# Second batch of state-space table products issued in the norm after the first FFN instead of in that FFN's last chunk

## The chip, the cores and the metric

The kernel runs on one core of a Trainium2 chip. The metric is the device time of one execution in microseconds; lower is better. Within 0.2% (2.4 us of 1207.69) counts as no change.

## The reference, cut to what matters

A decoder of four layers works on 256 positions of 1024 channels in float32. Each layer is a mixer and a norm, then an FFN and a norm. The mixers are attention, a state-space layer (S5), pooling, attention. The change touches the end of layer 0 (its FFN and the norm behind it) and the start of layer 1 (S5).

```
for i in range(DEPTH):
    m = mixer_i(h)                       # i = 1: s5_mixer
    h = layer_norm(DN_ALPHA * h + m, ln_g[i, 0], ln_b[i, 0])
    h = layer_norm(DN_ALPHA * h + swiglu(h, w1[i], w3[i], w2[i]), ln_g[i, 1], ln_b[i, 1])

# s5_mixer: u = x @ w_in, 64 groups of 16 channels, 64 complex states per group
#   h_t = lam * h_(t-1) + B u_t ;  y_t = Re(C h_t) + D u_t ;  gelu ; GLU with w_glu
```

## The kernel before

Each float32 matmul against weights is done as three products of reduced-precision halves. A weight tile of 128x1024 (512 KB) comes by DMA into one of four `raw` buffers, ScalarE (ACT) rounds it to its high half (`hi`), VectorE (DVE) subtracts to get the low half (`lo`), and TensorE (PE) uses both. The tiles are numbered in the order of use. SyncE (SP) issues their loads in this order in one program: the load of tile c waits until the low half of tile c-4 is made (`w_lo`). All engines run fixed programs, written by hand and synchronised by semaphores; nothing is scheduled at run time.

S5 works on blocks of eight positions. What happens inside a block is one 128x128 matrix (a Toeplitz block) per group, and these 64 matrices are computed by the kernel from the S5 parameters while the FFN of layer 0 runs. The last step of that is `m_half(h)`, for h = 0 and 1: 64 pairs of small products on PE make the first block rows of 32 groups in two PSUM banks; ACT copies both to `Msb[h]` (h = 0 in `slot3`, h = 1 in `lam`); `s5_diagonal` on DVE adds the D term and raises `m_d`. Then each of the eight block rows is stored to DRAM (`toep`) from Msb, 4 x 2 DMAs for each row: GpSimd (POOL) issues 40 of them (rows 0 to 4), SP issues 24 (rows 5 to 7). SP does this inside its sequence of tile loads: after the load of the tile S0+5 it waits for `m_d`, issues its 24 stores, and only then the loads of tiles S0+6 and S0+7 (S0 is the first of S5's eight `w_in` tiles) and then the moves of u described below. Much later the blocks are loaded back as `toepA` and `BT`.

The norm behind the FFN (n = 1, function `ln`) handles the 256 positions as two halves m = 0 and 1 of 128. DVE adds the residual from the accumulator banks (banks 0 and 1 for m = 0, banks 2 and 3 for m = 1), takes statistics and writes `x_tm`; PE transposes it (`turn_x`) into banks 4 to 7; ACT and DVE make the high and low halves `xboth`. S5 begins inside the norm: PE multiplies tiles S0 and S0+1 with m = 0, has then to wait for the second half's `x_tm`, and goes on with `turn_x(n, 1, (0, 1))`. The remaining tiles S0+2 to S0+7 follow (`u_tile(i)`, tile S0+i; i from 4 on writes banks 2 and 3). The result u is regrouped by four DMAs for each half h (two from ACT, two from SP, called `u_moves`), then `u_turned` goes on with it.

In the trace the lines are: L1783 and L1784 the products of `m_half` on PE, L696 its copies on ACT, L1366, L1370, L1372 `s5_diagonal` on DVE, L569 and L440 the stores on POOL and SP, L431 the loads of the `w_in` tiles on SP, L595 and L974 the high and low halves of a tile, L1571 `turn_x`, L1936, L1937, L1942 the products of `u_tile`, L389 `u_moves`, L795 and L1386 the copies behind them, L1955 `u_turned`, L1967 the next batch of 64 products.

Of the kernel before, what the change touches and what calls it, by code (L numbers as in the profile page):

```python
# [23 lines left out]
ALU = mybir.AluOpType  # L24
# [3 lines left out]
P = 128  # L28
# [7 lines left out]
FCH = D_FF // P  # L36
# [61 lines left out]
def build(nc, t, layers=DEPTH, last_ffn=True):  # L98
# [38 lines left out]
    with ExitStack() as ctx:  # L137
# [3 lines left out]
        def sem(name):  # L141
            return ctx.enter_context(nc.semaphore(name))
# [122 lines left out]
        def up_half(n, m):  # L265

            return bank[4 + m] if after_fox(n) else bank[m]

        def nth(n, m, b):

            return 8 * (n + 1) + 4 * m + b + 1
# [9 lines left out]
        later_landed, x_landed, bglu_landed = sem("later_landed"), [sem("x0_landed"), sem("x1_landed")], sem("bglu_landed")  # L281
        ones_set, bhi_sb, blo_sb = sem("ones_set"), sem("bhi_sb"), sem("blo_sb")
        up1_lo, up3_lo, up1_sum = sem("up1_lo"), sem("up3_lo"), sem("up1_sum")
        sub_done, zeros_set = sem("sub_done"), sem("zeros_set")
        var_ready, std_ready = sem("var_ready"), sem("std_ready")
        xn_ready = [sem("xn0_ready"), sem("xn1_ready")]
# [82 lines left out]
        def _(sp):  # L369
# [54 lines left out]
            for c in range(RAW, n_tiles):  # L424
                sp.wait_ge(w_lo, c - RAW + 1)
                for dst, src in LATER.get(c - KC - RAW, []):
                    sp.dma_start(dst, src).then_inc(later_landed, 16)
                if T1 <= c < T1 + KC:

                    h, k = (c - T1) // 4, T1 + 2 * ((c - T1) % 4)  # L430
                    sp.dma_start(raw[:, c % RAW, :].rearrange("p (k d) -> p k d", k=2),  # L431
                                 t["w"][k:k + 2, :, h * HALF:(h + 1) * HALF].rearrange("k p d -> p k d")).then_inc(raw_landed[c % RAW], 16)
                else:
                    sp.dma_start(raw[:, c % RAW, :], t["w"][tile_at(c)]).then_inc(raw_landed[c % RAW], 16)
                if c == T1 + RAW + 1:
                    sp.wait_ge(m_d, 1)
                    for s in range(5, STEP):
                        for j in range(4):
                            for h in range(2):
                                sp.dma_start(*toep_block(s, j, h)).then_inc(m_st_sp, 16)  # L440
                if c == T1 + 4 + RAW:
                    u_moves(0)
                if c == T1 + KC + RAW - 1:
                    u_moves(1)
                    toep_moves(T1)
# [5 lines left out]
        def _(pool):  # L451
# [87 lines left out]
            for l in range(layers):  # L539
                kind = MIXERS[l]  # L540
                if kind == "fox":


                    if l > 0:
                        pool.wait_ge(xn_ready[1], 2 * 2 * l)
                        nc.gpsimd.tensor_copy(
                            qa_of(1)[HD:KQ, :, :], cst[HD:KQ, C_HOT:C_HOT + HEADS].unsqueeze(2).to_broadcast([HEADS, HEADS, SEQ])
                        ).then_inc(qa_rows, 1)
                    if l == 0 and layers > 1:
                        s5_parameters()  # L550
                        step(nc.gpsimd.memset(slot[2][:, 0:D], 0.0))
                        for k in range(8):
                            pool.dma_start(t["toep"][:, k * D:(k + 1) * D], slot[2][:, 0:D]).then_inc(zero_st, 16)
                        pool.wait_ge(zero_st, 16 * 8)
                for k in range(2):

                    if kind == "s5" and k == 0:
                        pool.wait_ge(y_ps, 4)
                    if n > 0:
                        pool.wait_ge(xn_ready[1], 2 * n)  # L560
                    for q in range(2):
                        pool.dma_start(gb[:, q, :], t["ln_row"][q, n].partition_broadcast(P)).then_inc(gb_landed, 16)  # L562
                    if n == 1 and layers > 1:
                        s5_turns()
                        pool.wait_ge(m_d, 1)
                        for s in range(5):
                            for j in range(4):
                                for h in range(2):
                                    pool.dma_start(*toep_block(s, j, h)).then_inc(m_st, 16)  # L569
                    n += 1  # L570

# [2 lines left out]
        def _(act):  # L574
# [38 lines left out]
            def opening():  # L613

                for b in range(4):
                    for m in range(TM):
                        high(-1, m, b)
                    hi_to(min(b, 2))

            def ln(n, ahead, table, last_gate=None):  # L620

                nc.scalar.preload_act_table(ACT.Sqrt)
# [13 lines left out]
                    nc.scalar.preload_act_table(table)  # L636
                for b in range(4):
                    high(n, 1, b)

            def ffn(l, n):  # L640
                T0 = starts[l] + MIX_TILES[MIXERS[l]]
# [47 lines left out]
                        act.wait_ge(wb_ps, 2 * b + i + 1)  # L689
                        nc.scalar.copy(BT[:, 8 * b + 4 * i:8 * b + 4 * i + 4, :], bank[6 + i][:, :].rearrange("p (g n) -> p g n", g=4)).then_inc(bt_sb, 1)  # L690

                def m_half(h):

                    for i in range(2):
                        act.wait_ge(m_ps, 2 * h + i + 1)
                        nc.scalar.copy(Msb[h][:, 4 * i:4 * i + 4, :], bank[6 + i][:, :].rearrange("p (g n) -> p g n", g=4)).then_inc(m_sb, 1)  # L696

                s5_here = l == 0 and layers > 1
                act.wait_ge(up_ps, l + 1)
                silu_half(0)  # L700
# [10 lines left out]
                for c in range(2, FCH):  # L711
                    chunk(c)
                    if s5_here and 5 <= c < 13:
                        bt_block(c - 5)
                    if s5_here and c >= FCH - 2:
                        m_half(c - FCH + 2)
                split_to(top)

            def fox(l, f):
# [231 lines left out]
        def _(dve):  # L951
# [29 lines left out]
            def residual(n, m, j, src):  # L981

                if n > 0:
                    dve.wait_ge(xn_ready[m], 2 * n)
                cols = slice(j * HALF, (j + 1) * HALF)
                step(V.scalar_tensor_tensor(x_tm[:, m, cols], x_tm[:, m, cols], ALPHA, src, ALU.mult, ALU.add))

            def measure(m, j):
# [19 lines left out]
            def ln(n, last_tile, ahead, glu=None):  # L1008
# [68 lines left out]
                if between:  # L1077
                    for b in range(4):
                        low(n, 1, b)
                    lo_to(ahead)  # L1080

            def ffn(l, n):
# [73 lines left out]
                for c in range(2, FCH):  # L1156
                    chunk(c)
                if tables_here:
                    s5_diagonal()
                split_to(top)  # L1160

            def fox(l, f):
# [195 lines left out]
                        else:  # L1358
                            mark(ins)

            def s5_diagonal():

                tD = slot[0][:, 0:SEQ].rearrange("p (g c) -> p g c", g=16)
                dve.wait_ge(tables, 1)
                dve.wait_ge(turns, 1)
                mark(V.tensor_tensor(tD, dcol[:, :].unsqueeze(2).to_broadcast([P, 16, GC]),  # L1366
                                     cst[:, C_ID16:C_ID16 + GC].unsqueeze(1).to_broadcast([P, 16, GC]), ALU.mult))
                dve.wait_ge(m_sb, 4)
                marked()
                mark(V.tensor_tensor(Msb[0][:, :, 0:GC], Msb[0][:, :, 0:GC], tD[:, 0:8, :], ALU.add))  # L1370
                marked()
                V.tensor_tensor(Msb[1][:, :, 0:GC], Msb[1][:, :, 0:GC], tD[:, 8:16, :], ALU.add).then_inc(m_d, 1)  # L1372

            def s5(l, n):
                T0 = starts[l]
# [180 lines left out]
        def _(pe):  # L1556
# [132 lines left out]
            def zero_products(b, times):  # L1689

                for _ in range(times):
                    mm(bank[b][:, 0:SEQ], turn_sb[:, 0, 0:P], turn_sb[:, 0, 0:SEQ], start=True, stop=True)

            def ffn(l, n):
                T0 = starts[l] + MIX_TILES[MIXERS[l]]
                E0 = FCH * l
# [71 lines left out]
                            ins = nc.tensor.transpose(bank[6 + i][:, g * P:(g + 1) * P], BT[:, 8 * b + 4 * i + g, :], ident)  # L1768
                        ins.then_inc(wb_ps, 1)

                def m_half(h):

                    pe.wait_ge(tables, 1)
                    pe.wait_ge(bt_sb, 16)
                    if h == 1:
                        pe.wait_ge(m_sb, 2)
                    for i in range(2):
                        b = 2 * h + i
                        for q in range(4):
                            for j in range(4):  # L1780
                                g = 16 * j + 4 * b + q
                                lhs = slot[1][:, g * GC:g * GC + 32]
                                mm(bank[6 + i][32 * j:32 * j + 32, q * P:q * P + GC], lhs, CA[:, g, :], start=True, stop=True)  # L1783
                                ins = mm(bank[6 + i][32 * j:32 * j + 32, q * P + GC:(q + 1) * P], lhs,  # L1784
                                         CT[:, g, 0:STEP - 1, :].rearrange("p d c -> p (d c)"), start=True, stop=True)
                        ins.then_inc(m_ps, 1)

                s5_here = l == 0 and layers > 1
                pe.wait_ge(w_lo, T0 + 4)
                up_both(0).then_inc(up_ps, 1)  # L1790
# [7 lines left out]
                for c in range(3, FCH):  # L1798
                    up1(c)
                    up3(c)  # L1800
                    if c < FCH - 3:
                        down(c - 1)
                    if s5_here and 5 <= c < 13:
                        bt_block(c - 5)
                    if s5_here and c >= FCH - 2:
                        m_half(c - FCH + 2)
                down(FCH - 4)
                t, h = T0 + T_FFN - 3, FCH - 3

# [114 lines left out]
            def s5(l, n):  # L1924
# [115 lines left out]
                for m in range(TM):  # L2040
                    for i in range(2):
# [4 lines left out]
                        if i == 0:  # L2046
                            turn_x(n, m, (2, 3))
                    if m == 0:
                        turn_x(n, 1, (0, 1))
                for i in range(2, KC):  # L2050
                    u_tile(i)
                pe.wait_ge(ug0_sb, 1)
                pe.wait_ge(ug1_sb, 1)
# [220 lines left out]
```

## Time and profile before

| | us |
|---|---|
| median of 3 runs | 1207.69 (1207.59 to 1207.75) |
| the profiled execution | 1208.1 |
| its span, first to last instruction | 1206.3 |
| PE busy | 1172.1 (97% of the span) |
| DVE busy | 881.8 (73%) |
| ACT busy | 635.0 (53%) |
| POOL busy | 145.3 (12%) |

The profiled execution lies 0.4 us above the median, and 1.8 us of it lie outside the span. The profile lists instructions with start and duration on each engine, and for an engine that sat idle, what released it. Times in the rows are us from the start of the span. PE's matmuls overlap, so the distance between the starts of two of them is what one costs.

### The profile page before, as it was taken

Reading aid. Unit: us, or ns where it says so; the run is one execution under the profiler, and the core shown is the slowest. Engines: PE = TensorE matmul, PEld = TensorE weight load, DVE = VectorE, ACT = ScalarE, POOL = GpSimd, SP = SyncE. Lnnn points to the kernel's source line nnn. Section 1 sums busy time; section 2 is a strip of 40 time slices with the busy share of each in tenths; the row PEclk is TensorE's granted clock in tenths of the full one; section 3 lists DMA queues with packets and bytes.
Section 4 is the critical chain, followed back from the end, with each engine's and each line's share of the span. In section 5 each row is a group of like instructions: output and inputs, shape, how many; then the busy total and the mean of one; then the engine's idle time right before and its main releaser. Section 6 shows DMA issues by size and latency. Waiting matters only on the chain.

```text
span 1206.3 us, 18971 instructions
## 1 busy us (share of the span) xinstructions
PE 1172.1 (97%) x7386; PEld 1004.9 (83%) x7386; DVE 881.8 (73%) x1412; ACT 635.0 (53%) x1069; POOL 145.3 (12%) x187
## 2 busy tenths in 40 slices
PE   9999999999988999999998999999999999999996
PEld 7887899999967778888887888888878977888885
DVE  6779889889776677665668887666686767766655
ACT  5766445454435366555554556554538654654552
POOL 0640079101650000000000000000010000000000
PEclk9999999999999999999999999999999999999998
DMA  6684465655588556756654647666636433866550
GB/s 232 209 294 158 155 194 158 192 164 186 182 173 235 190 174 205 231 183 189 196 185 142 207 138 246 193 189 193 189 126 205 128 106 122 261 193 192 182 168 35
DMA packets 66513, 220.17 MB, mean 183 GB/s; under 512 B 11124, under 2 KB 12660, under 8 KB 65912
## 3 DMA queue, kind: packets, MB, share of 16 engines
q1 hardware_dynamic: 60536, 202.47, 53.1%
q0 software_dynamic: 4736, 14.55, 4.1%
q10 hardware_dynamic: 1152, 1.93, 0.7%
q8 instruction: 59, 0.97, 0.3%
q14 instruction: 30, 0.25, 0.1%
HBM read 210.28 MB, written 7.60 MB: 181 GB/s over the span
## 4 chain that ended last, share of the span: by engine, by line
PE 85%; DVE 9%; ACT 3%; DMA 2%; issue 1%; SPq 0%; ACTq 0%; DVEq 0%
PE bank L1599 18%; PE bank L1602 9%; PE bank L1614 9%; PE bank L1616 9%; PE bank L1620 9%; PE bank L1591 5%; PE bank L1593 5%; PE bank L1592 5%; PE bank L1651 4%; PE bank L1706 4%; DVE wlo L974 1%; PE bank L1571 1%; DVE ext L974 1%; DMA slot<-slot 1%; DVE x_tm L1032 1%
## 5 line engine op out<-in xcount | busy, mean ns | idle before, releaser
L974 DVE TENSOR_TENSOR wlo<-raw,whi 128x1024 fp32r<-128x1024 f32 x227 | 285.1, 1263 | 51.2 <-ACT whi L595 48.8
L595 ACT ACTIVATE whi<-raw 128x1024 fp32r<-128x1024 f32 x227 | 239.1, 1058 | 46.9 <-DMA raw<-in_w 26.8
L974 DVE TENSOR_TENSOR ext<-raw,ext 128x1024 fp32r<-128x1024 f32 x142 | 173.7, 1230 | 36.4 <-ACT ext L595 33.8
L1599 PE MATMUL bank<-xboth,whi 128*128 128x512 f32 x480 | 170.0, 397 | 0.0
L1599 PE MATMUL bank<-xboth,ext 128*128 128x512 f32 x480 | 168.7, 394 | 0.0
L595 ACT ACTIVATE ext<-raw 128x1024 fp32r<-128x1024 f32 x142 | 149.1, 1058 | 22.9 <-DMA raw<-in_w 16.2
L1591 PE MATMUL bank<-xboth,whi 128*128 128x256 f32 x496 | 142.1, 286 | 0.0
L1592 PE MATMUL bank<-xboth,whi 128*128 128x256 f32 x496 | 140.3, 283 | 0.0
L1593 PE MATMUL bank<-xboth,wlo 128*128 128x256 f32 x496 | 140.3, 283 | 0.0
L1602 PE MATMUL bank<-xboth,ext 128*128 128x256 f32 x480 | 124.6, 280 | 0.0
L1602 PE MATMUL bank<-xboth,wlo 128*128 128x256 f32 x480 | 124.2, 279 | 0.0
L1599 PEld LDWEIGHTS bank<-xboth,whi 128*128 128x128 f32 x480 | 88.4, 188 | 17.6 <-issue 0.3
L1599 PEld LDWEIGHTS bank<-xboth,ext 128*128 128x128 f32 x480 | 88.4, 188 | 16.4
L1591 PEld LDWEIGHTS bank<-xboth,whi 128*128 128x128 f32 x496 | 94.9, 191 | 1.7 <-issue 1.2
L1592 PEld LDWEIGHTS bank<-xboth,whi 128*128 128x128 f32 x496 | 95.0, 191 | 0.5
L1593 PEld LDWEIGHTS bank<-xboth,wlo 128*128 128x128 f32 x496 | 94.9, 191 | 0.0
L1602 PEld LDWEIGHTS bank<-xboth,wlo 128*128 128x128 f32 x480 | 90.5, 189 | 5.0
L1602 PEld LDWEIGHTS bank<-xboth,ext 128*128 128x128 f32 x480 | 90.4, 188 | 5.0
L663 ACT COPY cosT<-bank 128x256 f32<-128x256 f32 x60 | 22.3, 372 | 131.0 <-PE bank L1599 130.6
L1117 DVE TENSOR_TENSOR silu<-bank,cosT 128x256 f32<-128x256 f32 x60 | 25.4, 423 | 89.4 <-ACT cosT L663 89.2
L562 POOL DMA_DIRECT2D slot<-in_ln_row x16 | 8.6, 543 | 542.4 <-DVE x_tm L1044 472.4
L1614 PE MATMUL bank<-whi,hhi 128*128 128x512 f32 x196 | 61.0, 392 | 0.0
(396 smaller groups left out, 2329.7 us busy)
## 6 DMA issues: line engine op xcount, KB each, us to landing
raw<-in_w SPq DMA_DIRECT2D x370, 512.0 KB, 4.3
slot<-in_ln_row POOLq DMA_DIRECT2D x16, 512.0 KB, 5.0
toep<-slot POOLq DMA_DIRECT2D x8, 512.0 KB, 9.2
toepA<-toep SPq DMA_DIRECT2D x2, 1024.0 KB, 10.0
BT<-toep SPq DMA_DIRECT2D x2, 1024.0 KB, 7.3
slot<-in_s_B SPq DMA_DIRECT2D x2, 512.0 KB, 5.4
slot<-in_s_C SPq DMA_DIRECT2D x2, 512.0 KB, 4.6
x_tm<-in_x SPq DMA_DIRECT2D x1, 512.0 KB, 5.1
```

The lines of the kernel that those rows point to most:

```text
L595: nc.scalar.activation(hi_of(c), raw[:, c % RAW, :], ACT.Copy).then_inc(w_hi, 1)
L974: V.tensor_tensor(lo_of(c), raw[:, c % RAW, :], hi_of(c).bitcast(F32), ALU.subtract).then_inc(w_lo, 1)
L1591: mm(dst, wh, bhi[:, kc, :], start=(i == 0), stop=False)
L1592: mm(dst, wh, blo[:, kc, :], start=False, stop=False)
L1593: ins = mm(dst, wl, bhi[:, kc, :], start=False, stop=(i == len(chunks) - 1))
L1599: return mm(dst[:, :], hi_of(c)[:, kc * P:(kc + 1) * P], xboth[:, kc, :, :].rearrange("p a t -> p (a t)"), start=kc == 0, stop=kc == KC - 1)
L1602: return mm(dst[:, 0:SEQ], lo_of(c)[:, kc * P:(kc + 1) * P], xhi[:, kc, :], start=False, stop=False)
L1614: mm(banks[2 * m + j][:, :], a_hi[:, cols], hi_of(c)[:, j * HALF:(j + 1) * HALF], start=first, stop=False)
L1616: mm(banks[2 * m + j][:, :], a_hi[:, cols], lo_of(c)[:, j * HALF:(j + 1) * HALF], start=False, stop=False)
L1620: ins = mm(banks[2 * m + j][:, :], a_lo[:, cols], hi_of(c)[:, j * HALF:(j + 1) * HALF], start=False, stop=last)
L1651: return mm(banks[b][:, :], (a_lo if lo_act else a_hi)[:, cols], (lo_of if lo_w else hi_of)(c)[:, half], start=False, stop=stop)
L1706: return mm(out, x[:, kc, m * P:(m + 1) * P], w[:, 0:4, kc * P:(kc + 1) * P], start=start, stop=stop)
```

## The change

`m_half(1)` and all that hangs on it move. On PE its 64 pairs of products leave the last chunk of the FFN and stand between the last product of tile S0+1 with m = 0 and the transposes of the second half. They write banks 2 and 3 instead of 6 and 7, and wait for a new semaphore, `acc_read`, which DVE raises when it has read the second half's sums out of these banks. On ACT the two copies move behind the second of the four copies of `xboth` of the second half. On DVE the addition of the D term for h = 1 moves to the end of the norm. POOL's 40 stores are ordered by h, the first 20 behind `m_d` 1 and the other 20 behind `m_d` 2. SP's 24 stores wait for `m_d` 2, which is now raised by the moved addition; before, `m_d` 1 was raised when both halves were done. `u_tile(4)` also waits for the copies on ACT (`m_sb` 4).

```diff
+        def m_bank(h, i):
+
+            return bank[6 + i] if h == 0 else bank[2 + i]
...
                 if c == T1 + RAW + 1:
-                    sp.wait_ge(m_d, 1)
+                    sp.wait_ge(m_d, 2)
                     for s in range(5, STEP):
                         for j in range(4):
                             for h in range(2):
...
                         s5_turns()
-                        pool.wait_ge(m_d, 1)
-                        for s in range(5):
-                            for j in range(4):
-                                for h in range(2):
+                        for h in range(2):
+                            pool.wait_ge(m_d, h + 1)
+                            for s in range(5):
+                                for j in range(4):
                                     pool.dma_start(*toep_block(s, j, h)).then_inc(m_st, 16)
...
                 for b in range(4):
                     high(n, 1, b)
+                    if n == 1 and layers > 1 and b == 1:
+                        m_half(1)
...
-                    if s5_here and c >= FCH - 2:
-                        m_half(c - FCH + 2)
+                    if s5_here and c == FCH - 2:
+                        m_half(0)
...
+                if n == 1 and m == 1 and layers > 1:
+                    V.scalar_tensor_tensor(x_tm[:, m, cols], x_tm[:, m, cols], ALPHA, src, ALU.mult, ALU.add).then_inc(acc_read, 1)
+                    dve.wait_ge(acc_read, j + 1)
+                    return
...
                     for b in range(4):
                         low(n, 1, b)
+                    if n == 1 and layers > 1:
+                        s5_diagonal(1)
                     lo_to(ahead)
...
+            def m_half(h):
+
+                pe.wait_ge(tables, 1)
+                pe.wait_ge(bt_sb, 16)
+                for i in range(2):
+                    if h == 1:
+                        pe.wait_ge(acc_read, i + 1)
...
                     if m == 0:
+                        m_half(1)
                         turn_x(n, 1, (0, 1))
                 for i in range(2, KC):
+                    if i == 4:
+                        pe.wait_ge(m_sb, 4)
                     u_tile(i)
```

On PE, between tile S0+1 (its halves are in `far_hi` and `far_lo`) and the transposes of the second half, the order before is:

```order
L1942 MATMUL bank0<-far_hi,xboth 128x512 [waits xT_ready]
L1942 MATMUL bank0<-far_hi,xboth 128x512
L1571 MATMUL bank4<-cst,x_tm 128x128 [waits xT_ready,xn1_ready]
L1571 MATMUL bank4<-cst,x_tm 128x128
L1571 MATMUL bank5<-cst,x_tm 128x128 [waits xT_ready]
```

And with the change (the lines are twelve further on in its file here):

```order
L1954 MATMUL bank0<-far_hi,xboth 128x512 [waits xT_ready]
L1954 MATMUL bank0<-far_hi,xboth 128x512
L1718 MATMUL bank2<-slot3,slot1 32x16 [waits acc_read,bt_sb,tables]
L1719 MATMUL bank2<-CT,slot1 32x112
...
L1718 MATMUL bank3<-slot3,slot1 32x16
L1719 MATMUL bank3<-CT,slot1 32x112
L1583 MATMUL bank4<-cst,x_tm 128x128 [waits xT_ready,xn1_ready]
L1583 MATMUL bank4<-cst,x_tm 128x128
```

The 128 small products, 64 pairs, now stand between the two, in banks 2 and 3.

On DVE, the additions before stand together ahead of the norm, and the end of the norm (the low halves of `xboth`, then those of tiles S0+2 to S0+5) has none:

```order
L1366 TENSOR_TENSOR slot0<-dcol,cst 128x256 [waits turns,tables,hlo_ready]
L1370 TENSOR_TENSOR slot3<-slot3,slot0 128x8x16 [waits dve_own,m_sb]
L1372 TENSOR_TENSOR lam<-lam,slot0 128x8x16 [waits dve_own]
L974 TENSOR_TENSOR wlo<-raw,whi 128x1024 [waits w_hi]
...
L996 TENSOR_TENSOR xboth<-bank7,xboth 128x2x128 [waits xhi_ready]
L974 TENSOR_TENSOR wlo<-raw,whi 128x1024 [waits w_hi] x4
L1380 COPY slot0<-bank1 128x512 [waits w_used]
```

With the change:

```order
L1380 TENSOR_TENSOR slot0<-dcol,cst 128x256 [waits turns,tables,hlo_ready]
L1384 TENSOR_TENSOR slot3<-slot3,slot0 128x8x16 [waits dve_own,m_sb]
L981 TENSOR_TENSOR wlo<-raw,whi 128x1024 [waits w_hi]
...
L1007 TENSOR_TENSOR xboth<-bank7,xboth 128x2x128 [waits xhi_ready]
L1384 TENSOR_TENSOR lam<-lam,slot0 128x8x16 [waits dve_own,m_sb]
L981 TENSOR_TENSOR wlo<-raw,whi 128x1024 [waits w_hi] x4
L1392 COPY slot0<-bank1 128x512 [waits w_used]
```

The addition for h = 1, into `lam`, is now behind the last low half of `xboth` and ahead of tile S0+2's low half.

On SP nothing changes places; with the change its rows from the six loads S0 to S0+5 to the first moves of u are (the first and the last of the 24 stores shown):

```order
L436 DMA raw<-in_w 128x2x512 [waits w_lo] x6
L445 DMA toep<-slot3 16x8x48 [waits m_d]
L445 DMA toep<-lam 16x8x48
...
L445 DMA toep<-lam 16x8x16
L436 DMA raw<-in_w 128x2x512 [waits w_lo] x2
L439 DMA raw<-in_w 128x1024 [waits w_lo]
L394 DMA slot4<-slot0 16x8x256 [waits u1_sb]
L394 DMA slot4<-slot0 16x8x256
```

What moved is the point of the program at which its `m_d` wait is met: it is now released by the addition into `lam` at its new place.

## Rows read from the trace of the kernel before

**Rows 1.** Page, part 4: shares of the chain that ended last.

```profile
PE 85%; DVE 9%; ACT 3%; DMA 2%; issue 1%; SPq 0%; ACTq 0%; DVEq 0%
```

**Rows 2.** Timeline of PE (start us, us, engine, line, operation), the batch h = 1 and what follows.

```profile
323.81 0.26 PE L1783 MATMUL bank<-slot 128*32 128x16 f32 x7
...
326.07 0.73 PE L1614 MATMUL bank<-whi,hhi 128*128 128x512 f32 x2
...
330.31 0.39 PE L1651 MATMUL bank<-whi,h4hi 128*128 128x512 f32 x1
```

**Rows 3.** Timelines of DVE and ACT, end of the FFN to start of the norm.

```profile
325.88 1.23 DVE L974 TENSOR_TENSOR wlo<-raw,whi 128x1024 fp32r<-128x1024 f32 x1
...
327.88 0.29 DVE L1372 TENSOR_TENSOR lam<-lam,slot 128x128 f32<-128x128 f32 x1
...
332.55 0.68 DVE L986 SCALAR_TENSOR_TENSOR x_tm<-x_tm,bank 128x512 f32<-128x512 f32 x1
...
325.76 1.05 ACT L696 COPY lam<-bank 128x512 f32<-128x512 f32 x2
329.18 1.06 ACT L595 ACTIVATE whi<-raw 128x1024 fp32r<-128x1024 f32 x1 [2.37 <-PE bank L1620]
```

**Rows 4.** Timelines of PE and ACT in the norm and in the tiles behind it.

```profile
341.19 0.63 PE L1942 MATMUL bank<-far_hi,xboth 128*128 128x512 f32 x2
344.03 0.66 PE L1571 MATMUL bank<-cst,x_tm 128*128 128x128 f32 x4 [2.21 <-DVE x_tm L1044]
...
349.49 0.50 PE L1936 MATMUL bank<-whi,xboth 128*128 128x512 f32 x1 [0.77 <-DVE wlo L974]
...
360.54 0.39 PE L1936 MATMUL bank<-whi,xboth 128*128 128x512 f32 x1
...
365.53 0.61 PE L1942 MATMUL bank<-whi,xboth 128*128 128x512 f32 x2
...
347.13 0.66 ACT L605 ACTIVATE xboth<-bank 128x256 fp32r<-128x256 f32 x2 [1.96 <-PE bank L1571]
```

**Rows 5.** Timeline of SP's queue (start, time to issue, transfer).

```profile
333.07 0.74 SPq L440 DMA_DIRECT2D toep<-slot  x1
...
342.49 0.43 SPq L440 DMA_DIRECT2D toep<-lam  x1
...
352.07 0.94 SPq L431 DMA_DIRECT2D raw<-in_w  x2
...
356.02 1.34 SPq L389 DMA_DIRECT2D slot<-slot  x2
```

**Rows 6.** Timelines of DVE and ACT: halves of tiles S0+2 to S0+6.

```profile
348.22 4.62 DVE L974 TENSOR_TENSOR wlo<-raw,whi 128x1024 fp32r<-128x1024 f32 x4
...
357.41 1.23 DVE L974 TENSOR_TENSOR wlo<-raw,whi 128x1024 fp32r<-128x1024 f32 x1 [1.42 <-ACT whi L595]
...
356.31 1.06 ACT L595 ACTIVATE whi<-raw 128x1024 fp32r<-128x1024 f32 x1 [1.79 <-DMA raw<-in_w]
```

**Rows 7.** The chain that ended last, in order of time, 356 to 384 us.

```profile
356.73 9.71 DMA slot<-slot
...
367.57 1.95 PE bank L1955 x32
...
370.15 3.11 PE bank L1967 x64
...
382.82 1.89 PE bank L1967 x64
```

**Rows 8.** Windows (us, then busy time of PE, PEld, DVE, ACT, POOL, PE's granted clock, DMA share, GB/s).

```profile
342.00:344.00 2.00, 0.00 (x0) 0.00 (x0) 1.96 (x6) 0.29 (x1) 2.00 (x5) 1.00 0.69 131
...
370.00:372.00 2.00, 2.00 (x49) 1.92 (x52) 0.40 (x1) 0.79 (x2) 0.00 (x0) 0.66 1.22 138
372.00:374.00 2.00, 2.00 (x28) 1.61 (x21) 0.94 (x2) 1.26 (x3) 0.00 (x0) 0.50 1.06 201
...
1200.00:1202.00 2.00, 0.00 (x0) 0.00 (x0) 1.90 (x5) 0.29 (x1) 0.00 (x0) 0.52 0.23 94
```

More of the change, by code:

```diff
@@ L283, in build @@
         up1_lo, up3_lo, up1_sum = sem("up1_lo"), sem("up3_lo"), sem("up1_sum")
+        acc_read = sem("acc_read")
         sub_done, zeros_set = sem("sub_done"), sem("zeros_set")
@@ L618, in opening @@
                     hi_to(min(b, 2))
+            def m_half(h):
+                for i in range(2):
+                    act.wait_ge(m_ps, 2 * h + i + 1)
+                    nc.scalar.copy(Msb[h][:, 4 * i:4 * i + 4, :], m_bank(h, i)[:, :].rearrange("p (g n) -> p g n", g=4)).then_inc(m_sb, 1)
             def ln(n, ahead, table, last_gate=None):
@@ L690, in bt_block @@
                         nc.scalar.copy(BT[:, 8 * b + 4 * i:8 * b + 4 * i + 4, :], bank[6 + i][:, :].rearrange("p (g n) -> p g n", g=4)).then_inc(bt_sb, 1)
[L692 to L696, printed above, removed]
                 s5_here = l == 0 and layers > 1
@@ L1158, in ffn @@
                 if tables_here:
-                    s5_diagonal()
+                    s5_diagonal(0)
                 split_to(top)
@@ L1359, in s5_tables, with s5_diagonal @@
                             mark(ins)
-            def s5_diagonal():
+            def s5_diagonal(h):
                 tD = slot[0][:, 0:SEQ].rearrange("p (g c) -> p g c", g=16)
[L1364 to L1368, printed above, removed]
+                if h == 0:
+                    dve.wait_ge(tables, 1)
+                    dve.wait_ge(turns, 1)
+                    mark(V.tensor_tensor(tD, dcol[:, :].unsqueeze(2).to_broadcast([P, 16, GC]),
+                                         cst[:, C_ID16:C_ID16 + GC].unsqueeze(1).to_broadcast([P, 16, GC]), ALU.mult))
+                dve.wait_ge(m_sb, 2 * h + 2)
                 marked()
-                mark(V.tensor_tensor(Msb[0][:, :, 0:GC], Msb[0][:, :, 0:GC], tD[:, 0:8, :], ALU.add))
-                marked()
-                V.tensor_tensor(Msb[1][:, :, 0:GC], Msb[1][:, :, 0:GC], tD[:, 8:16, :], ALU.add).then_inc(m_d, 1)
+                V.tensor_tensor(Msb[h][:, :, 0:GC], Msb[h][:, :, 0:GC], tD[:, 8 * h:8 * h + 8, :], ALU.add).then_inc(m_d, 1)
             def s5(l, n):
@@ L1692, in zero_products, with m_half @@
                     mm(bank[b][:, 0:SEQ], turn_sb[:, 0, 0:P], turn_sb[:, 0, 0:SEQ], start=True, stop=True)
+            def m_half(h):
+                pe.wait_ge(tables, 1)
+                pe.wait_ge(bt_sb, 16)
+                for i in range(2):
+                    if h == 1:
+                        pe.wait_ge(acc_read, i + 1)
+                    b = 2 * h + i
+                    for q in range(4):
+                        for j in range(4):
+                            g = 16 * j + 4 * b + q
+                            lhs = slot[1][:, g * GC:g * GC + 32]
+                            mm(m_bank(h, i)[32 * j:32 * j + 32, q * P:q * P + GC], lhs, CA[:, g, :], start=True, stop=True)
+                            ins = mm(m_bank(h, i)[32 * j:32 * j + 32, q * P + GC:(q + 1) * P], lhs,
+                                     CT[:, g, 0:STEP - 1, :].rearrange("p d c -> p (d c)"), start=True, stop=True)
+                    ins.then_inc(m_ps, 1)
             def ffn(l, n):
@@ L1769, in bt_block @@
                         ins.then_inc(wb_ps, 1)
[L1771 to L1786, printed above, removed]
                 s5_here = l == 0 and layers > 1
@@ L1804, in ffn @@
                         bt_block(c - 5)
-                    if s5_here and c >= FCH - 2:
-                        m_half(c - FCH + 2)
+                    if s5_here and c == FCH - 2:
+                        m_half(0)
                 down(FCH - 4)
```

## The prediction

> **What bounds the kernel now.** I first read the page's chain that ended last: PE holds most of it [rows 1]. So an instruction taken from a place where PE is busy is worth its time, as long as what follows is ready earlier too, and a wait added on PE costs its full length. The change touches only the stretch from 323 to about 373 us, so I next read the timelines of that stretch engine by engine, and last its chain. Three things are to be seen. At 323.81 us the batch h = 1 runs with PE busy before and after it [rows 2]. In the norm PE stands still for 2.21 us before the transposes of the second half, since it needs DVE's x_tm [rows 4]. And SP, between its loads of tiles S0+5 and S0+6, is occupied with its 24 stores from 333.07 to 352.07 us [rows 5].
>
> **The batch leaves the FFN.** From its first product to the next matmul it takes 326.07 - 323.81 = 2.26 us [rows 2]. Is what follows ready that much earlier? The last tile of the FFN is wanted at 330.31, then 328.05; its low half ends at 325.88 + 1.23 = 327.11 and doesn't depend on the batch [rows 2, 3]. 0.94 us are left. The norm's first step on DVE, at 332.55, follows on the halves of S0 and S0+1, and the first of these was released by a PE product at 329.18 [rows 3], so it comes 2.26 us earlier too. **-2.26 us**, for everything up to the transposes.
>
> **The batch enters the norm.** The last two products of S0+1 with m = 0 run from 341.19 to 341.82; such a product is 0.39 long, so they start about 0.23 apart and make room at 341.65; the transposes start at 344.03 [rows 2, 4]. That is 2.38 us for 2.26 us of work. The sums of the second half have been read by then, because what PE waits for at 344.03 lies several DVE steps behind them. So **0** on PE. If the cover were gone it would cost 2.26 us, and the bounds here are 0 and about +0.2 (start of a small product after a large one).
>
> **ACT's copies.** They take 1.05 us [rows 3] and stand ahead of the xboth copy of 347.13, before which ACT idled 1.96 us [rows 4]. **0.** Without this cover 1.05 would be paid.
>
> **DVE's addition.** 0.29 us [rows 3]. Before, it lay in an idle of DVE ahead of the norm. Now it stands right ahead of the low halves from 348.22, of which the first releases PE at 349.49 after a wait [rows 4, 6]. **+0.29 us.** Tile S0+2 then starts at 349.49 - 2.26 + 0.29 = 347.52, and I call -1.97 us the gain so far.
>
> **SP's wait.** This is the term that decides. m_d 2 is raised at the end of the norm: 348.22 - 2.26 + 0.29 = 346.25, against a wait that was met without delay at 333.07 before [rows 5, 6]. Queued behind it on SP are the 24 stores, the loads of tiles S0+6, S0+7 and the next one, and u_moves. The 24 issues took 19.0 us before: the first 7 took 9.42 us, to 342.49, and the other 17 took 9.58 us, 0.564 each, to 352.07 [rows 5]. The first seven stood right behind the loads of S0+4 and S0+5, which will be over by 346 us. POOL's issues go on beside SP's in both. I take the second rate: 24 x 0.564 = 13.5 us. The bounds are the bare 0.43 and a gap of 0.05 (11.5 us) and the whole 19.0 us.
> The load of S0+6 is then issued at 346.25 + 13.5 = 359.8. Before, from its issue at 352.07 to the end of its low half at 357.41 + 1.23 = 358.64 it took 6.57 us [rows 5, 6]. So the tile is ready at 366.4. PE wants it at 360.54 - 1.97 = 358.6 [rows 4]. **PE waits 7.8 us** where before the tile had 1.9 us to spare. Tiles S0+6 and S0+7 take 5.45 us, from 360.54 to 366.0 (the last two start at 365.53, 0.23 apart) [rows 4], so PE is through at 371.8, and u_turned starts at about 372.0. Before it started at 367.57, because it waited for the moves of u [rows 7]. **+4.4 us** at this point. From there S5 is one chain, and nothing in it is set by a clock of its own; SP's second u_moves, the loads of toepA and POOL's stores all stand within the same shift.
>
> **TensorE's clock.** After 2.2 us without a matmul the granted clock stayed at 1.00 (2.4 GHz) [rows 8]. After PE's last matmul, with nothing for several us, it fell to half (1.2 GHz) by 1200 to 1202 us [rows 8]. And before the S5 chain it fell for some 3.4 us between 370 and 374 us, behind a short idle and small transposes [rows 8]; there 64 products took 3.11 us against 1.89 us later [rows 7]. A wait of 7.8 us should let it fall. For up to 3.4 us PE then works at half speed and loses up to 1.7 us. On the other side the idle ahead of u_turned is gone, and I assume that the fall at 370 us goes with it, -1.2 us (3.11 - 1.89). **+0.5 us** net; the bounds are -1.2 and +1.7.
> The Trainium skill, page "TensorE: Matmul & The Clock Gate", section "HAM oscillation — how this bites in real kernels", says that a wait for a DMA between two groups of matmuls can bring the clock down to half, so that the next group starts slow. By that rule the tiles behind the wait are slow and the sum ends at +4.9 or above; without it, at +3.2 to +4.4. The trace agrees as far as its idle at the very end shows the fall, but no wait for a tile of this length stands in it.
>
> **Sum.** -2.26 and +0.29 are inside the +4.4 already: 4.4 + 0.5 = +4.9 us. On the span that is 1206.3 + 4.9 = 1211.2, with 1.8 us outside it 1213.0 for the profiled execution, and since that one lay 0.4 above the median, 1207.69 + 4.9 = **1212.6 us**.
>
> **The rivals.**
> 1. *The stores issue faster and the clock is kind.* At 0.48 us each the tile is 2.0 us less late, +2.4 us at u_turned; if also no slow stretch follows, or the old one vanishes without a new one, +1.2. That is 1208.9 to 1210.1, and mostly within 0.2%. For it: seventeen issues included only one long one. Against it: POOL will be storing its largest blocks just then. 0.14.
> 2. *The tile is not late, and the change gains.* Then PE keeps -1.97 us: 1205.7 us. It decides at the point where SP gets through its 24 stores by 358.6 - 6.57 = 352.0, in 5.7 us or 0.24 us each. The fastest row is 0.43 [rows 5]. It would take a route of the tile that is far shorter than 6.57 us, or a u_turned that is released so much sooner that it pays. Nothing in the profile speaks for it beyond my own reading of the order. 0.08.
> 3. *The moves of u end last.* u_moves is issued behind three tile loads, at about 361.3, and if it takes its 9.71 us again [rows 7] and the copy behind it 1.1, u_turned starts at 372.1 to 373, +4.6 to +5.5, and with slow products more; some 1213 us. For it: the row of 9.71 us is on the chain now. Against it: in it the moves from ACT and more tile loads ran at the same time, and these will be apart. 0.13.
> 4. *SP's issues are as slow as before, 19.0 us:* +5.5 on top, 1218.1 us. For it: the first seven. Against it: no tile load runs beside them. 0.05.
> The forecast, SP held at a middling rate, has 0.60.
>
> **How the numbers follow.** Cases 3, 4 and the forecast are slower by more than 0.2% (73 + 5 = 0.78), case 1 is mostly no change (0.14), case 2 is faster (0.08). The range runs from the middle of case 1, 1209.3, to near case 4, 1217.0; that leaves out case 2, half of 1 and most of 4.
>
> **What would show it.** The batch L1783/L1784 (under new line numbers) in the idle before the transposes, and these at 341.8 us: right on the first two steps. The addition at 346 us, SP's first store directly behind it and the load of S0+6 near 360 us: right on SP. PE idle before the first product of u_tile(6), some 8 us, released by DVE's low half, and a granted clock of half in the window behind it. u_turned near 372 to 374 us. I would be wrong if the load of S0+6 is issued before 353 us, or if the 24 issues take a third of the time that I give them.

## The result and the profile after

The changed kernel takes 1216.26 us (median of 6 runs, 1215.5 to 1218.74), the kernel before 1207.64 us (6 runs, 1203.97 to 1207.97): ratio 1.0077, 95% interval 1.0060 to 1.0093. It is slower by 8.6 us. Forecast were 1212.6 us and a range of 1209.3 to 1217.0. The profiled execution took 1216.19 us with a span of 1214.4, 8.1 above that of before.

The page's chain that ended last (answers to [rows 1]); SP's queue has come into it:

```profile
PE 84%; DVE 9%; ACT 3%; issue 1%; SPq 1%; DMA 1%; DVEq 0%; ACTq 0%
```

The timeline of PE (answers to [rows 2, 4]):

```profile
338.66 0.63 PE L1954 MATMUL bank<-far_hi,xboth 128*128 128x512 f32 x2
339.22 0.26 PE L1718 MATMUL bank<-slot 128*32 128x16 f32 x7
...
341.50 0.66 PE L1583 MATMUL bank<-cst,x_tm 128*128 128x128 f32 x4
...
347.16 0.50 PE L1948 MATMUL bank<-whi,xboth 128*128 128x512 f32 x1 [0.97 <-DVE wlo L981]
...
368.62 0.79 PE L1948 MATMUL bank<-whi,xboth 128*128 128x512 f32 x1 [10.30 <-DVE wlo L981]
...
376.18 1.95 PE L1967 MATMUL bank<-cst,slot 32*128 32x32 f32 x32
```

The batch fills the idle of the norm, and the transposes behind it start 2.53 us earlier than before with no wait. Tile S0+2 starts 2.33 us earlier. Then PE stands still for 10.30 us ahead of S0+6, and u_turned, the last row, starts 8.61 us later than in [rows 7].

DVE, ACT and POOL (answers to [rows 3, 6]):

```profile
330.04 0.68 DVE L997 SCALAR_TENSOR_TENSOR x_tm<-x_tm,bank 128x512 f32<-128x512 f32 x1
...
345.69 0.28 DVE L1384 TENSOR_TENSOR lam<-lam,slot 128x128 f32<-128x128 f32 x1
346.26 10.32 POOL L574 DMA_DIRECT2D toep<-lam  x20 [7.80 <-DVE lam L1384]
...
366.25 1.06 ACT L600 ACTIVATE whi<-raw 128x1024 fp32r<-128x1024 f32 x1 [14.10 <-DMA raw<-in_w]
367.34 1.23 DVE L981 TENSOR_TENSOR wlo<-raw,whi 128x1024 fp32r<-128x1024 f32 x1 [13.73 <-ACT whi L600]
```

SP's queue (answers to [rows 5]), the 24 stores L445 and the load of S0+6, L436:

```profile
346.00 0.35 SPq L445 DMA_DIRECT2D toep<-slot  x1
...
352.96 1.09 SPq L445 DMA_DIRECT2D toep<-lam  x1
354.10 1.66 SPq L445 DMA_DIRECT2D toep<-slot  x1
...
361.82 0.43 SPq L445 DMA_DIRECT2D toep<-lam  x1
362.29 0.94 SPq L436 DMA_DIRECT2D raw<-in_w  x2
```

The first store follows at once on the addition of 345.69. While POOL issues its second twenty, from 346.26 to 356.58, SP's issues take up to 1.66 us; from 357.56 on they take 0.43. The 24 together take 362.29 - 346.00 = 16.3 us.

The chain that ended last shows the same stretch as one path, and what comes at its end (answers to [rows 7]):

```profile
362.29 3.94 DMA raw<-in_w
366.25 1.06 ACT whi L600
367.34 1.24 DVE wlo L981
368.62 0.79 PE bank L1948
...
389.82 3.53 PE bank L1979 x64
```

The windows (columns as in [rows 8]):

```profile
350.00:352.00 2.00, 2.00 (x10) 1.68 (x9) 0.51 (x1) 0.44 (x1) 2.00 (x5) 1.00 0.91 139
...
362.00:364.00 2.00, 0.00 (x0) 0.00 (x0) 0.00 (x0) 0.00 (x0) 0.00 (x0) 0.61 0.31 39
...
370.00:372.00 2.00, 2.00 (x6) 1.54 (x5) 0.58 (x1) 0.90 (x1) 0.00 (x0) 0.50 1.13 124
372.00:374.00 2.00, 2.00 (x8) 1.59 (x8) 1.81 (x2) 0.75 (x2) 0.00 (x0) 0.83 0.94 317
...
390.00:392.00 2.00, 2.00 (x44) 1.85 (x40) 1.87 (x5) 0.27 (x2) 0.00 (x0) 0.50 0.00 0
```

The granted clock is still 1.00 (2.4 GHz) in the first windows of the wait, falls to half (1.2 GHz) from 362 us on, and is back between 372 and 374 us: S0+6 and S0+7 take from 368.62 to 376.1, 7.5 us against 5.45 before. It falls once more at 390 us.

### The profile page after: what moved, and what is told of

Its sections match the earlier page's. It is cut to its first block, busy times and chain, and to the rows that moved or that the text cites. A ratio compares the mean times of both kernels' runs of the same rounds, so it can differ in the third digit from the quotient of the medians.

```text
span 1214.4 us, 18973 instructions
## 1 busy us (share of the span) xinstructions
PE 1173.3 (97%) x7386; PEld 1005.6 (83%) x7386; DVE 881.6 (73%) x1412; ACT 635.2 (52%) x1069; POOL 145.4 (12%) x187
## 4 chain that ended last, share of the span: by engine, by line
PE 84%; DVE 9%; ACT 3%; issue 1%; SPq 1%; DMA 1%; DVEq 0%; ACTq 0%
PE bank L1611 18%; PE bank L1614 9%; PE bank L1626 9%; PE bank L1628 9%; PE bank L1632 9%; PE bank L1603 5%; PE bank L1605 5%; PE bank L1604 5%; PE bank L1663 4%; PE bank L1735 4%; DVE wlo L981 2%; SPq L445 1%; PE bank L1583 1%; DVE ext L981 1%; DMA raw<-in_w 1%
```

## The experiments

The theory: all of the loss comes from SP's `m_d` wait at the end of the norm, which holds the load of S0+6 behind 24 issues; the place of the batch on PE is a gain. Rivals: the batch in the norm costs something itself; the wait for the tile is harmless and the clock behind it is the cost; the moves of u end last.

The table has each kernel's median, and from its profiled execution the start of tile S0+2, PE's idle ahead of S0+6, the start of u_turned, and as a last mark the start of the late batch, the 64 products that read `BT` as loaded back from `toep` (in before L2002 at 397.83). Each ratio compares with the kernel before as it was measured beside that run: 1207.64 us for the change, 1207.71 for e1 to e4, 1207.40 for e5 and e6, 1208.07 for e7 to e9, 1206.50 for e10 and e11. Kernels of one such group are best compared with each other, the others by their ratios.

| | median us | ratio to before, 95% | S0+2 | idle | u_turned | late batch |
|---|---|---|---|---|---|---|
| before | 1207.64 | | 349.49 | 0 | 367.57 | 397.83 |
| the change | 1216.26 | 1.0077 (1.0060 to 1.0093) | 347.16 | 10.30 | 376.18 | 406.46 |
| e1 | 1203.59 | 0.9966 (0.9954 to 0.9977) | 347.57 | 0 | 364.12 | 394.37 |
| e9, e1 again | 1202.67 | 0.9953 (0.9935 to 0.9970) | 347.67 | 0 | 364.21 | 392.86 |
| e8 | 1206.51 | 0.9987 (0.9974 to 1.0000) | 350.66 | 0 | 367.19 | 395.85 |
| e11, e8 again | 1205.94 | 0.9992 (0.9978 to 1.0007) | 350.41 | 0 | 366.95 | 395.60 |
| e10 | 1205.08 | 0.9986 (0.9970 to 1.0001) | 349.42 | 0 | 365.96 | 396.16 |
| e2 | 1209.09 | 1.0011 (0.9997 to 1.0024) | 347.50 | 0 | 364.05 | 398.07 |
| e5 | 1209.21 | 1.0013 (1.0002 to 1.0025) | 347.30 | 4.27 | 370.86 | 399.52 |
| e6, one execution | 1215.46 | | 347.25 | 6.16 | 372.48 | 402.75 |
| e7 | 1215.85 | 1.0061 (1.0045 to 1.0076) | 347.21 | filled, 1.47 | 375.22 | 405.47 |
| e4 | 1218.95 | 1.0093 (1.0074 to 1.0112) | 347.25 | filled, 0 | 381.09 | 410.95 |
| e3 | 1220.93 | 1.0105 (1.0087 to 1.0123) | 350.97 | 11.21 | 381.54 | 410.20 |

**e1 and e9, the wait taken off SP.** The change, but POOL issues all 64 stores and SP none:

```diff
-                if c == T1 + RAW + 1:
-                    sp.wait_ge(m_d, 2)
...
                             pool.wait_ge(m_d, h + 1)
-                            for s in range(5):
+                            for s in range(STEP):
```

> The change, but POOL issues all 64 stores and SP none, so that no tile load stands behind a wait for m_d. Theory (SP's order): the load of S0+6 goes out by 348 us, PE doesn't wait for that tile, and the gain in front shows: 1207.6 - 2.3 = 1205.3 us, down to 1204 if the moves of u, now with nothing ahead of them on SP, also land earlier. Rival (the stores themselves, as DMA traffic of the wrong moment, keep the tile back): the tile's way from issue to low half grows by several us and the time stays above 1210.

> The kernel of e1_pool_stores_all again, beside e8 on one chip: 1203.6 us if the first measurement holds.

The two timelines of e9, SP's and PE's:

```profile
326.03 23.11 SPq L435 DMA_DIRECT2D raw<-in_w  x6
...
347.67 0.50 PE L1940 MATMUL bank<-whi,xboth 128*128 128x512 f32 x1 [0.98 <-DVE wlo L974]
...
364.21 1.94 PE L1959 MATMUL bank<-cst,slot 32*128 32x32 f32 x32
```

SP's loads run through, no tile is late, and the kernel is faster than before in both sets of runs, though the 32 stores of h = 1 still go out behind `m_d` 2, now all from POOL (346.76 to 363.81 us in e9). Against the change u_turned starts 376.18 - 364.21 = 12 us earlier, and the late batch 406.46 - 392.86 = 13.6 us (12.1 in e1, in which a slow stretch is left); the medians lie 13.6 us (e9) and 12.7 us (e1) apart. So SP's wait, with all that it drags behind it, costs 12 us at u_turned.

**e8 and e11, the same edit without the batch's move.** The edit of e1 made to the kernel before, with its wait for `m_d` 1:

> The kernel before, batch h = 1 in the FFN as it was, only POOL issues all 64 stores. The rest of e1's gain then belongs to the batch's place. If the batch in the norm is worth 2.26 - 0.3 = 2 us, this is 2 us slower than e1 and 1 to 2 us faster than before (the moves of u, on PE's chain before, no longer collide with late tile loads): about 1206. Rival (all of e1's gain comes from SP's freed queue): as fast as e1, 1203.6.

> The kernel before with all 64 stores on POOL once more, for the comparison on the same chip: about 1206.5 us as before. If the fall of the clock behind the idle of the norm is regular, the window 344 to 346 us shows about 0.56 again; if it is a matter of chance, it may show 1.00 and then S0+2 starts near 349.5.

Freeing SP's queue alone brings the median 1.6 and 0.6 us below before, neither certain by its interval. What is left to the place of the batch, e9 against e8, is a gain of 3.0 us at u_turned and at the late batch, and of 3.8 us in the medians, whose intervals lie apart. So the batch in the norm costs nothing of its own. The steps had promised only 1.97. The missing us is already there at S0+2, which starts 350.66 - 347.67 = 3.0 us later in e8 than in e9. In the windows of e11 the clock fell behind the norm's idle:

```profile
342.00:344.00 2.00, 0.10 (x1) 0.10 (x2) 1.97 (x6) 0.29 (x1) 2.00 (x5) 1.00 0.51 82
344.00:346.00 2.00, 1.84 (x7) 1.28 (x8) 1.96 (x5) 0.77 (x2) 2.00 (x5) 0.56 0.50 76
346.00:348.00 2.00, 2.00 (x10) 1.51 (x8) 0.29 (x1) 0.00 (x0) 2.00 (x5) 0.59 0.46 68
```

The windows of e8 show the same, 0.56 and 0.59. In the profiled execution of before the clock stayed at 1.00 there, with the same 2.2 us of idle, and S0+2 started at 349.49.

**e10, that idle filled.** e8, and five constant products where the change puts its batch (`idle_products` is a helper that the kernel already has: products of a constant whose results nobody reads):

```diff
+                        pe.wait_ge(xT_ready, nth(n, 0, 0))
+                        idle_products(4, 256, 5)
                         turn_x(n, 1, (0, 1))
```

> The kernel before with all 64 stores on POOL, and five constant 128x256 products (0.43 us each as in the filled wait, 2.15 us) in PE's idle of 2.21 us of the norm, ahead of the second half's transposes. Nothing else moves. In the profiled run without them the granted clock fell to 0.56 and 0.59 between 344 and 348 us, and tile S0+2 started at 350.66 instead of 349.49. Theory (part of the gain of the batch's new place is that it keeps the clock up in this idle): the clock stays at 1.00 from 342 to 350 us, S0+2 starts at about 349.5, and the median lies about 1 us below that of the same kernel without the five. Rival (the start of S0+2 is set by DVE and the clock costs nothing, or the five products push the transposes): S0+2 at 350.7 or later, median equal or higher.

A window and the timeline of PE in e10:

```profile
344.00:346.00 2.00, 1.65 (x8) 1.04 (x8) 1.97 (x5) 0.66 (x2) 2.00 (x5) 1.00 0.48 73
```

```profile
341.57 2.32 PE L1679 MATMUL bank<-cst 128*128 128x256 f32 x10
...
349.42 0.50 PE L1928 MATMUL bank<-whi,xboth 128*128 128x512 f32 x1 [0.77 <-DVE wlo L967]
...
380.48 2.54 PE L1959 MATMUL bank<-BT,slot 128*32 128x128 f32 x64
```

The clock holds and S0+2 starts 0.99 us earlier than in e11. So 1 of the 3 us of the batch's place is the clock that it keeps up; the rest, 349.42 - 347.67 = 1.75 us from e10 to e9, is what the steps priced at 1.97. At the end the us is not kept: a slow stretch stands at 380 us, where e11's same batch took 1.95, and the late batch starts 0.56 later than in e11. The medians differ by 0.9, less than their intervals resolve.

**e3, the wait alone.** The batch is put back into the FFN on PE and ACT; DVE's addition, and the waits of SP and POOL, stay as changed:

```diff
-            return bank[6 + i] if h == 0 else bank[2 + i]
+            return bank[6 + i]
...
-                    if s5_here and c == FCH - 2:
-                        m_half(0)
+                    if s5_here and c >= FCH - 2:
+                        m_half(c - FCH + 2)
```

> Only the late m_d: PE and ACT make the batch h = 1 in the FFN's last chunk as before, but DVE adds its D term at the end of the norm, and SP and POOL wait as in the change. Theory (SP's order): all of the loss without the gain of 2.3 us in front, so the span is 8.1 + 2.3 = 10.4 us above before: about 1218 us, with PE idle for 10 us before the first product of S0+6. Rival (the batch's new place on PE costs): near 1207.6.

The end of SP's 24 stores and PE:

```profile
366.69 0.94 SPq L436 DMA_DIRECT2D raw<-in_w  x2
...
373.35 0.80 PE L1946 MATMUL bank<-whi,xboth 128*128 128x512 f32 x1 [11.21 <-DVE wlo L979]
```

The loss is there without the batch's move, and larger than the forecast of 1218: the chain is that of the change, and SP's first store comes 3.8 us later (349.81), since the norm ends later with the batch in the FFN and the clock at 0.51 to 0.64 between 344 and 348 us. The batch's place on PE is therefore no part of the loss.

**e2 and e5, SP's stores split.** In both, SP issues its 12 stores of h = 0 at the old place, behind `m_d` 1. The 12 of h = 1 stand behind the first u_moves in e2, and ahead of the load of S0+6 in e5 (shown):

```diff
-                    sp.wait_ge(m_d, 2)
+                    sp.wait_ge(m_d, 1)
                     for s in range(5, STEP):
                         for j in range(4):
-                            for h in range(2):
-                                sp.dma_start(*toep_block(s, j, h)).then_inc(m_st_sp, 16)
+                            sp.dma_start(*toep_block(s, j, 0)).then_inc(m_st_sp, 16)
+                    sp.wait_ge(m_d, 2)
+                    for s in range(5, STEP):
+                        for j in range(4):
+                            sp.dma_start(*toep_block(s, j, 1)).then_inc(m_st_sp, 16)
```

> The change, but SP issues the 12 stores of h = 0 at the old place behind m_d 1, and the 12 of h = 1 behind the first moves of u. Theory: nothing that PE waits for is behind the late m_d; 1204 to 1206 us. Rival (stores as traffic): the 12 late stores and POOL's twenty run beside the tile loads and the moves of u and delay them; 1207 us or more.

> The change, but SP issues the 12 stores of h = 0 at the old place behind m_d 1; then m_d 2 and the 12 of h = 1 stand ahead of the load of S0+6. Theory (a price for each store that SP issues behind m_d 2, 16.3/24 = 0.68 us): the load goes out 8.1 us after 346.0, at 354.1, the tile is ready at 360.4 instead of 368.6, PE idles 2 us in place of 10.3, and the clock doesn't fall; the moves of u go out at 355.7 as before and bind again: about 1207 us. Rival (the wait itself, not the count behind it, costs): near 1216.

SP's queue in e2, and its chain that ended last:

```profile
355.80 6.94 SPq L450 DMA_DIRECT2D toep<-lam  x12
362.79 1.39 SPq L439 DMA_DIRECT2D raw<-in_w  x3
```

```profile
365.47 9.90 DMA slot<-slot
```

e2 has e1's u_turned, 364.05, and loses it behind: the twelve stores hold three tile loads back until 362.79, these go out right ahead of the second moves of u, which then take 9.90 us; PE waits 2.40 us for them, and slow stretches follow. I had overlooked the loads queued behind those twelve, and the forecast of 1204 to 1206 us failed by it. In e5 the queue and PE are:

```profile
346.14 8.04 SPq L448 DMA_DIRECT2D toep<-lam  x12
354.23 1.51 SPq L436 DMA_DIRECT2D raw<-in_w  x2
...
362.74 0.80 PE L1951 MATMUL bank<-whi,xboth 128*128 128x512 f32 x1 [4.27 <-DVE wlo L984]
```

Half as many issues, 8.1 us as forecast, and the wait goes down from 10.30 to 4.27, not to the 2 that I expected. The tile itself needed 8.5 us from its issue, where the change's needed 6.3; with 6.3 the wait would have been 2. POOL's last stores, issued up to 356.72, ran beside it here; that they are the reason is not shown. The clock fell to 0.50 behind this shorter wait too, where I had expected it to hold.

**e6, POOL's second twenty behind SP's stores.** It tells whether SP's issues are slow by nature or by POOL's stores:

```diff
                             pool.wait_ge(m_d, h + 1)
+                            if h == 1:
+                                pool.wait_ge(m_st_sp, 16 * 24)
```

> The change, but POOL's second twenty stores wait until SP's 24 have landed. It separates the two prices of an issue on SP. If SP's issues are slowed by POOL's blocks in flight, the 24 take 24 x 0.48 = 11.5 us in place of 16.3 and the load of S0+6 goes out at 357.5 instead of 362.3; if they are slow by themselves they still take 16 us. The time is not the question (POOL's blocks come some 17 us later and may hold up the loads of the blocks).

SP's queue and a window in e6:

```profile
352.64 0.43 SPq L445 DMA_DIRECT2D toep<-slot  x1
...
357.88 0.94 SPq L436 DMA_DIRECT2D raw<-in_w  x2
```

```profile
350.00:352.00 2.00, 2.00 (x11) 1.65 (x10) 0.60 (x1) 0.34 (x1) 0.00 (x0) 1.00 0.30 42
```

The same 24 issues take 357.88 - 346.09 = 11.8 us instead of 16.3, twenty of them 0.43 or less. In the window from 350 the DMA engines are busy for 0.30 of the time, in the change for 0.91. The late batch starts 3.7 us earlier than in the change. The span of its one execution is only 0.7 shorter: the clock falls at 454 to 458 us (0.66 and 0.50) and at 926 to 930 us (0.50 and 0.72), where it stayed at 1.00 in the change, and behind the second place, at 941 us, 0.7 us of the lead are left.

**e4 and e7, the wait filled.** Constant products ahead of `u_tile(6)`, 40 in e4 and 22 in e7:

```diff
+                    if i == 6:
+                        idle_products(7, 256, 22)
```

> The change with 40 products of a constant, 128x256, ahead of the first product of S0+6 on PE; by the rows of the S5 part they take about 8.5 us of the 10.3 us that PE idles there. Theory: the wait for the tile stays, but the clock doesn't fall in it, and tiles S0+6 and S0+7 take 5.5 us, not 7.6: about 2 us faster than the change, 1214.2; 1212.6 if the slow stretch of the second batch of states at 389 us goes too. Rival (the slow products are slow from something else, a DMA or operand contention): no faster than the change.

> The change with 22 products of a constant ahead of the first product of S0+6. e4 showed that one of them is two passes and takes 0.43 us, so that its 40 took 17.4 us and pushed PE's start past the tile; 22 take 9.4 of the 10.3 us of idle. Theory: the clock stays at 1.00 there, S0+6 and S0+7 take 5.5 us in place of 7.5, 2 us faster than the change: about 1214. Rival (something else slows these products): as the change.

In e4 the 40 were too many: at 0.43 us each they took 17.43 us and pushed S0+6 to 375.35, so that the kernel gained nothing over the change. Its clock stayed at 1.00, and S0+6 and S0+7 took 5.7 us. (One of its 6 executions took 4137.57 us, for which nothing here gives a reason; the median in the table is of the other five.) In e7 they fit. The timeline of PE and a window of e7:

```profile
358.22 9.66 PE L1699 MATMUL bank<-cst 128*128 128x256 f32 x44
369.36 0.50 PE L1948 MATMUL bank<-whi,xboth 128*128 128x512 f32 x1 [1.47 <-DVE wlo L981]
...
377.72 3.09 PE L1979 MATMUL bank<-BT,slot 128*32 128x128 f32 x64
```

```profile
370.00:372.00 2.00, 2.00 (x11) 1.62 (x10) 0.61 (x1) 0.41 (x1) 0.00 (x0) 1.00 1.18 117
```

The clock stays at 1.00, and S0+6 and S0+7 take 5.6 us instead of 7.5. So the clock behind the wait costs 1.9 us at this place. At u_turned 1.0 of it is left, since the tile was ready 0.7 us later here, and at the late batch the same, with the slow stretch behind u_turned of [rows 7] back and the one at 390 us gone. In the medians a gain over the change is not certain: the ratios differ by 0.0016, about 2 us, and their intervals overlap.

## Why the prediction was right in kind and short in size

**Right.** The batch leaves the FFN: -2.26 forecast, DVE's first residual comes 2.51 us earlier (332.55 to 330.04). It enters the norm's idle at no cost; where the clock would fall in that idle, as in e8 and e11, it even earns 1 us (e10), but in the profiled execution of before the clock did not fall there. ACT's copies and DVE's addition: 0 and +0.29 forecast, S0+2 forecast at 347.52 and found at 347.16. SP's first store forecast at 346.25, found at 346.00. The tile from issue to low half: 6.57 forecast, 368.57 - 362.29 = 6.28 found. e1 and e9 show by taking it away that this wait, with the stores behind it, is the whole loss. Rival 3, the moves of u last, did not happen: PE came to u_turned without a wait. The tile was late, so rival 2 is out, and its 1205.7 us needed just what e1 does, a load of S0+6 that isn't held.

**Mis-sized: "24 x 0.564 = 13.5 us".** SP's issues took 16.3, inside the bounds 11.5 and 19.0. I took the rate of the last seventeen of [rows 5] and set the first seven aside as a matter of tile loads. In the change POOL issues its second twenty at just this time, from 346.26 on, and e6, in one execution, shows that they cost 16.3 - 11.8 = 4.5 us of the 16.3. I had said that POOL would be storing its largest blocks just then, and used it only against rival 1. This is +2.8 us at the load of S0+6, and PE's idle is 10.30 instead of 7.8 (SP's first store came 0.25 earlier and the tile's way was 0.29 shorter, but PE also got to the wait 0.36 earlier).

**Mis-sized: the clock, "+0.5 us net".** The first half, a loss of up to 1.7 behind the wait, was 2.0 (e7: 1.9). The second half failed in its kind: "I assume that the fall at 370 us goes with it, -1.2 us". It did go there, the batch behind u_turned took 1.95, but a slow stretch came up at the batch of 389.75, 3.60 against 1.96 before, and took the gain back (+1.6). The stretch is not tied to the idle ahead of u_turned: e7 has its slow batch behind u_turned with no idle ahead of it. e1 and e9, the same kernel, differ by little else, with 3.50 and 1.96 for the batch at 377.8 and 1.5 us at the late batch. What decides where it falls stays open.

**The sum.** At u_turned 4.4 + 1.7 = +6.1 was forecast and +8.6 found. Of the 2.5 between them 2.5 are the longer idle and 0.3 the clock, less 0.3 of small terms. What S5 then gained at its first batch (-1.6: the next u_turned is 6.99 later than before) and lost at its second (+1.6) cancels, so +8.6 stands at the late batch and in the medians, against the 4.9 forecast. The 3.7 us between them are these 2.5 and the 1.2 that were booked as a gain of the clock. The time lies in the stated range by 0.7 us, near the end that was set by rival 4's slow issues and not by the forecast's own sum. Rival 1 fell with its rate of 0.48 us for each issue. Rival 4, with 19.0 us and 1218.1, missed the 16.3 by as much as my forecast did, from the other side, and was nearer in the time; its chance of 0.05 was too low.

The Trainium skill, page "TensorE: Matmul & The Clock Gate", section "HAM oscillation — how this bites in real kernels", had a wait for a DMA between groups of matmuls bring the clock to half. The trace agrees: 0.50 (1.2 GHz) behind 10.30 us of idle in the change and behind 4.27 us in e5.

## What to carry to other kernels

When a step that feeds a store is moved later, look at the queue that issues the store before looking at the engine that computes: every load behind a semaphore wait on that queue moves with it, and here that turned a gain of 3 us into a loss of 9. If the step's place is good, give the stores to a queue that has nothing urgent behind them (here POOL's, with all 64 stores on it: 0.9966 and 0.9953 of the time before). Price a row of issues with the transfers of the new place beside it, and don't book the disappearance of a slow clock stretch as a gain.

## What the runs showed of the hardware that was not expected

- An issue on SP took 0.43 us (0.47 from one to the next) where the DMA engines were lightly loaded, share 0.30 to 0.37 in e6, and 0.69 to 1.66 us at shares of 0.84 to 0.93 with POOL issuing beside it in the change. POOL's issuing alone did not slow it: in before the issues took 0.43 us mostly at 342 to 347 us with POOL issuing all along (share 0.69 to 0.72), after 1.5 us each at 338 to 342 (share 0.99 in the first window). A high share alone did not either: in e2, behind POOL's last issue, three issues at 358.5 to 360 us took 0.43 at shares of 1.13 and 0.96. Most of the slow issues fell where both came together; only POOL's part was tested by removal.
- An idle of 2.2 us in the norm was followed by a clock of 0.51 to 0.64 in e8, e11 and e3, and by 1.00 in before, around the same instructions. It cost 1 us at the next tile (e10 against e11).
- A float32 product of 128x256 constant data shows as two instructions and took 0.43 us, so 22 products are 44 instructions and 9.66 us (e7).
- A move of u of 128 KB took 9.7 us in before ([rows 7]), where three tile loads were issued in the 4 us ahead of it and three right behind it, and 9.9 us in e2, with three issued right ahead of it. Both times it was what PE waited for.
